# Keeping the low parts of the weights in DRAM instead of computing them again in every chunk

## The reference

```python
h = _layer_norm(x) * (1 + scale[:, None]) + shift[:, None]
proj = h @ w_in                                   # (2048, 1024) @ (1024, 2560)
xa, ga, u, v, gb = jnp.split(proj, SPLITS, axis=-1)
ya = _pool_mixer(xa, w_pool, pool_scale) * jax.nn.silu(ga)
yb = _sgu_mixer(gelu(u), gelu(v), sgu_ln_g, sgu_ln_b, w_sgu, b_sgu) * jax.nn.silu(gb)
y = jnp.concatenate([ya, yb], axis=-1) @ w_out    # (2048, 1024) @ (1024, 1024)
z = DEEPNORM_ALPHA * x + gate[:, None] * y
return _layer_norm(z) * ln_g + ln_b
```

## Time and profile before

| | us |
|---|---|
| median of 3 runs | 678.67 (677.87 to 679.04) |
| profiled execution, its own time | 678.93 |
| span of the profiled execution | 677.2 |
| TensorE busy | 664.5 |
| VectorE busy | 525.6 |
| ScalarE busy | 239.3 |

### The profile page before, as it was taken

How to read it: one execution, slowest core, us unless ns; L and a number is a source line. 1 busy time by engine, 2 the same in 40 slices (tenths; PEclk the granted TensorE clock), 3 DMA queues, 4 the chain that set the end, 5 groups by cost and what they waited for, 6 DMA issues and landing times.

```text
span 677.2 us, 8864 instructions
## 1 busy us (share of the span) xinstructions
PE 664.5 (98%) x3087; PEld 552.9 (82%) x3087; DVE 525.6 (78%) x973; ACT 239.3 (35%) x316; POOL 61.9 (9%) x77
## 2 busy tenths in 40 slices
PE   8999999999999999999999999999999999999995
PEld 7888787878888888888888888888888888888884
DVE  5879989859769868759969967776978977555876
ACT  4444434338213333326511333334721333323300
POOL 2000200100012101100002201000002210000010
PEclk9999999999999999999999999999999999999998
DMA  8993352883425442575324362288233463224011
GB/s 332 396 370 131 125 187 88 169 300 129 142 76 186 168 176 93 97 210 223 126 94 155 124 248 93 93 109 324 93 124 123 136 245 117 95 81 162 38 63 62
DMA packets 33976, 106.68 MB, mean 158 GB/s; under 512 B 6509, under 2 KB 7569, under 8 KB 33938
## 3 DMA queue, kind: packets, MB, share of 16 engines
q1 hardware_dynamic: 33938, 106.22, 47.6%
HBM read 97.80 MB, written 8.40 MB: 157 GB/s over the span
## 4 chain that ended last, share of the span: by engine, by line
PE 89%; DVE 5%; issue 3%; ACT 1%; DMA 1%; POOL 0%; SPq 0%; POOLq 0%; DVEq 0%; ACTq 0%
PE bank_b L1008 59%; PE bank_a L1008 26%; PE bank_a L1122 2%; DVE gate_rows L723 1%; DMA x_norm<-in_x 1%; PE bank_b L1068 1%; DVE x_stats L622 1%; PE bank_b L1032 0%; ACT h_high L476 0%; ACT w_high L466 0%; DVE w_low L601 0%; DVE y_low L829 0%; PE bank_b L1087 0%; PE bank_b L1059 0%; DVE mixed L818 0%
## 5 line engine op out<-in xcount | busy, mean ns | idle before, releaser
L1008 PE MATMUL bank_b<-h_high,w_high 128*128 128x512 f32 x512 | 202.1, 395 | 0.6 <-DVE sgu_bias L757 0.6
L1008 PE MATMUL bank_b<-h_low,w_high 128*128 128x512 f32 x512 | 199.4, 390 | 0.0
L1008 PE MATMUL bank_b<-h_high,w_low 128*128 128x512 f32 x512 | 199.4, 389 | 0.0
L466 ACT ACTIVATE w_high<-w_float 128x1024 fp32r<-128x1024 f32 x100 | 105.5, 1056 | 149.5 <-DMA w_float<-in_w_units 56.3
L601 DVE TENSOR_TENSOR w_low<-w_float,w_high 128x1024 fp32r<-128x1024 f32 x100 | 122.1, 1221 | 42.5 <-ACT w_high L466 42.3
L1008 PEld LDWEIGHTS bank_b<-h_high,w_high 128*128 128x128 f32 x512 | 96.2, 188 | 21.0 <-issue 1.8
L1008 PEld LDWEIGHTS bank_b<-h_high,w_low 128*128 128x128 f32 x512 | 96.1, 188 | 20.2
L1008 PEld LDWEIGHTS bank_b<-h_low,w_high 128*128 128x128 f32 x512 | 96.2, 188 | 19.7 <-issue 0.5
L411 POOL TENSOR_TENSOR z_rstd<-z_var_eps,minus_half 128x1 f32<-128x1 f32 x16 | 22.0, 1377 | 367.3 <-DVE z_var_eps L858 357.4
L1008 PE MATMUL bank_a<-w_high,y_high 128*128 128x512 f32 x128 | 49.8, 389 | 0.0
L1008 PE MATMUL bank_a<-w_low,y_high 128*128 128x512 f32 x128 | 49.8, 389 | 0.0
(11 more groups left out here) (180 smaller groups left out, 945.4 us busy)
## 6 DMA issues: line engine op xcount, KB each, us to landing
w_float<-in_w_units SPq DMA_DIRECT2D x104, 512.0 KB, 3.3
x_norm<-in_x SPq DMA_DIRECT2D x16, 512.0 KB, 4.4
z<-in_x SPq DMA_DIRECT2D x16, 512.0 KB, 5.5
out<-z SPq DMA_DIRECT2D x15, 512.0 KB, 4.7
z<-in_mod_units SPq DMA_DIRECT2D x12, 512.0 KB, 9.6
x_norm<-in_x_channels SPq DMA_DIRECT2D x12, 512.0 KB, 13.8
mod_spare<-in_mod_units SPq DMA_DIRECT2D x6, 512.0 KB, 8.2
x_norm<-in_w_units SPq DMA_DIRECT2D x4, 512.0 KB, 4.3
```

The costliest lines, as they stand in the source:

```text
L466: nc.scalar.activation(wH[:, n % S_SLOTS, :], wF[:, n % F_SLOTS, :], ACT.Copy).then_inc(w_high, 1)
L1008: last = mm(bank, wl if n == 2 else wh, ml if n == 1 else mh, start=start and n == 0, stop=stop and n == 2)
```

## The change

In chunk 0 VectorE still subtracts, and SP stores each of the 28 low parts to a new DRAM tensor `low_units` (`store_low`). In the other chunks SP loads the low part of unit n + 2 in step n straight into its slot of `wL` (`load_low`), and VectorE no longer subtracts there, except for units 20 to 27 of the last chunk, which are prepared as before. SP's load of a weight waits for ScalarE's `w_high_ready` instead of VectorE's `w_low_ready`, and TensorE waits for `w_high_ready` and for the landing. The table `LAST_SPLITS_IN`, the tiles and all products stay as they are.

```diff
+    low_units = nc.dram_tensor("low_units", [UNITS, P, D], F32).ap()
             def load_w(c, n):
-                wait(sp, w_low, c * UNITS + n - F_SLOTS + 1)
+                held = n - F_SLOTS
+                if isinstance(c, int) and c * UNITS + held < UNITS:
+                    wait(sp, w_low, held + 1)
+                elif isinstance(c, int) and c == CHUNKS - 1 and held >= IN_UNITS:
+                    sp.wait_ge(w_low, UNITS + held - IN_UNITS + 1)
+                else:
+                    sp.wait_ge(w_high, c * UNITS + held + 1)
                 sp.dma_start(wF[:, n % F_SLOTS, :], w_units[n % UNITS]).then_inc(w_landed[n % F_SLOTS], 16)
+            def store_low(n):
+                sp.wait_ge(w_low, max(n + 1, len(EARLY)))
+                stored = v_low_stored if n < V_UNITS else low_stored[n % S_SLOTS]
+                sp.dma_start(low_units[n], w_of(0, n)[1].bitcast(F32)).then_inc(stored, 16)
+
+            def load_low(c, n):
+                if n % UNITS < S_SLOTS:
+                    sp.wait_ge(low_stored[n % S_SLOTS], (UNITS // S_SLOTS - 1) * 16)
+                    if isinstance(c, int) and c == 0:
+                        sp.wait_ge(v_low_stored, V_UNITS * 16)
+                sp.wait_ge(unit_done, c * UNITS + n - S_SLOTS + 1)
+                sp.dma_start(wL[:, n % S_SLOTS, :].bitcast(F32), low_units[n % UNITS]).then_inc(low_landed[n % S_SLOTS], 16)
...
                         load_w(c, n + 2 * AHEAD)
+                    if first and V_UNITS < n < FIRST_LOOP:
+                        for unit in ((4, 5, 6, 7), (0, 1), (2, 3))[n - V_UNITS - 1]:
+                            store_low(unit)
+                    if first and FIRST_LOOP <= n + AHEAD < UNITS:
+                        store_low(n + AHEAD)
+                    if (first and n + AHEAD >= UNITS) or (not first and not last) or (last and n + AHEAD < IN_UNITS):
+                        load_low(c, n + AHEAD)
...
+                            if g == 0 and not first:
+                                act.wait_ge(z_stats, c * TILES)
...
             def split_low(c, n):
                 dve.wait_ge(w_high, c * UNITS + n + 1)
+                if isinstance(c, int) and c == 0:
+                    dve.wait_ge(low_stored[n % S_SLOTS], (n // S_SLOTS - 1) * 16)
...
-                    if not (last and n in LAST_SPLITS_IN):
+                    if first and n + AHEAD < UNITS:
                         split_low(c, n + AHEAD)
...
-                    pe.wait_ge(w_low, c * UNITS + n + 1)
+                    if first:
+                        pe.wait_ge(w_low, n + 1)
+                    else:
+                        pe.wait_ge(w_high, c * UNITS + n + 1)
+                        pe.wait_ge(low_landed[n % S_SLOTS], ((c - 1) * (UNITS // S_SLOTS) + n // S_SLOTS + 1) * 16)
```

More of the change, by code:

```diff
@@ L180, in hybrid_layer @@
         unit_done = sem("unit_done")
+        low_stored = [sem(f"w_low_stored{i}") for i in range(S_SLOTS)]
+        v_low_stored = sem("v_w_low_stored")
+        low_landed = [sem(f"w_low_landed{i}") for i in range(S_SLOTS)]
         vec_turned, vec_ready = sem("vec_turned"), sem("vec_ready")
@@ L828, in y_low @@
                 dve.wait_ge(high, c * G + g + 1)
+                if isinstance(c, int) and c == 0 and g == 0:
+                    dve.wait_ge(v_low_stored, V_UNITS * 16)
                 vec.tensor_tensor(yL[:, row, :], src[:, :], yH[:, row, :].bitcast(F32), ALU.subtract).then_inc(low, 1)
@@ L1248, in last_products @@
                             pe.wait_ge(ys_low, c * G + i + 1)
-                            pe.wait_ge(w_low, c * UNITS + IN_UNITS + i + 1)
+                            pe.wait_ge(w_low, UNITS + i + 1)
                         if half == 1 and j == 0:
```

## The result

The changed kernel takes 687.47 us (median of 4 runs, 685.36 to 688.33), the kernel before in the same session 678.86 us. The ratio is 1.0125, with a 95% interval of 1.0099 to 1.0151. The forecast was 680.7 with a range of 678.2 to 683.6: the sign is right, the size is not.

What follows compares the result with a forecast made beforehand. The prediction took TensorE as the bound, busy 98% of the span. To 678.93 us it added 0 for VectorE, 2.0 for unit 19 and 0 for chunk 0: 680.9 profiled, median 680.7, range 678.2 to 683.6.

Steps and rivals of the forecast that it cites:

- What is removed: 76 VectorE subtractions in chunks 1 to 3, 92.8 us of VectorE's work, give the span 0 us.
- Where it does not fit: Unit 19's low part, queued behind the scattered statistics stores, lands late in chunks 1 and 2: 2.0 us, bounds 1.3 to 3.8.
- I take 1.0 of the 1.28 us: Unit 20's weight lands before the stores, so the jam may move ahead by up to 1.28 us; 1.0 was counted.
- the upper bound: If unit 21's weight keeps its time, TensorE stalls at unit 19 for 2.3 us in chunk 1, 1.5 in chunk 2.
- the restart of TensorE: Starting TensorE again after the stall at unit 19 costs 0.1 us, twice.
- Chunk 0: A low-part store moves the jam back 1.28 us; y_pool's reserve before unit 20 is 2.5 us, so 0 was counted.
- signs of being wrong: No TensorE wait for the low part's landing, that wait away from units 19 and 20, or a chunk 0 y_pool wait.
- VectorE's waits for stores cost 0: VectorE's added waits are for stores four units old, which it finds past: 0 us.
- What is late next: Unit 20's low part comes 5.1 us after unit 19's, 0.3 us before it is needed: no second stall, no reserve.
- The pile-up: Rival: the queue drains slower, making unit 20's low part late: 684 us in the middle, 687.3 at the far end; chance 0.13.
- The stall: Main case: TensorE stalls at unit 19 in chunks 1 and 2; own range 680.0 to 683 us, chance 0.50.
- the hidden case: Rival: low parts are hidden everywhere, no loss: 678.7 us and up to 1.3 more; chance 0.33.

Runs made afterwards that it cites:

- experiment 1: The changed kernel without its stores and loads of low parts and the waits for them, multiplying by stale low parts: 678.45 us, ratio 1.0002.
- experiment 5: The kernel before plus chunk 0's 28 stores of low parts; none is loaded and VectorE subtracts in every chunk: 681.93 us, ratio 1.0036.
- experiment 6: The changed kernel with all four loads of x moved from step 16 to 17, behind unit 21's weight and unit 19's low part: 689.72 us, ratio 1.015.
- experiment 8: The changed kernel with the eight early low parts all stored in step 5 of chunk 0, none in steps 6 and 7: 690.21 us, ratio 1.0144.
- experiment 7: The changed kernel with eight unused matmuls ahead of TensorE's wait for unit 19's low part in chunks 1 and 2: 686.87 us, ratio 1.0103.

## Why the prediction was wrong

**What is removed: right.** 0 us for VectorE's subtractions (experiment 1).

**Where it does not fit: the right place, too small.** The term was 2.0 us, with bounds 1.3 and 3.8; the stalls are 3.6 and 1.4 us. The step that failed is "I take 1.0 of the 1.28 us": the room in front of the stores was taken as a gain for all that follows. The stores did land 0.6 and 2.8 us earlier against TensorE, but the weight of unit 21 did not, as the drain from their landing to its rounding grew by 1.9 and 2.7 us. In chunk 2 the weight kept its place, and the stall is 1.4 us, near the 1.5 of the upper bound. In chunk 1 it was 1.3 us later against TensorE than before: the upper bound "if that keeps its time" was no bound. The 0.78 MB that had moved less by 301 us account for the 1.9 us of chunk 1.

Why they were held up more is not settled. Before, the stores' writes ran beside the bytes of a weight issued at 283.46; here the queue had nothing left to move from 284.7 on, and the writes ran alone. That SP's issue blocks needs no low part: it took 10.73 us in experiment 1 too, and in chunk 2 of the changed kernel the four loads took 2.00 us and the one low part behind them 6.91. And the jam varies by itself: from the second store's issue to unit 21's rounding it is 18.4 to 20.3 us in the three kernels without loads of low parts (before, experiments 1 and 5, chunks 1 and 2), and 19.2 and 21.3 us in the changed one. A term worked out to tenths of a microsecond could not be had from one trace of it.

**A missing term: the clock.** 2.9 us behind the stall of chunk 1. The prediction priced the restart of TensorE at 0.1 us, by the wait of 1.0 us in the earlier trace rows. This held for the short waits (unit 19 of chunk 2: 5.69 for 5.46) and not for that of 3.4. Experiments 6 and 8 show the same fall behind 3.1, 3.4 and 4.0 us, experiment 7 none behind 1.3. Around 2 us it went either way: the clock fell a microsecond after the 2.1 us of experiment 6, and it didn't behind the 2.0 us of experiment 8's chunk 2 and the 2.2 and 2.5 us of experiment 7. So the length of the idle time alone doesn't decide it there. The Trainium skill's page "TensorE: Matmul & The Clock Gate", section "What's actually happening", says that the slow clock is the default and that activity releases it; this trace agrees, with 0.50 behind the long wait and 0.99 once TensorE has worked again for a while. The four executions of the changed kernel follow it too: from 688.33 us at a mean clock of 0.991 to 685.36 us at 0.998.

**Chunk 0: 0 was wrong, it cost 1.3 us.** It varies, too: the two waits are 4.7 us in the profile of experiment 7, whose chunk 0 is the same. The reserve of 2.5 us and the path through `y_pool` were right, and TensorE's wait for it is one of the signs of being wrong that the prediction named. What was mis-sized is the delay: the weight of unit 21 is 147.19 - 143.62 = 3.6 us late, not 1.28, and 3.6 - 2.5 = 1.1 us is the wait. Most of it is the jam itself: the second store of the statistics lands 14.5 us after its issue at 126.33, where before it took 11.2 from 125.74. "VectorE's waits for stores cost 0" held, as far as no wait of TensorE ends with one; what was missed is that stores ahead of weights in the same queue delay the weights, and lengthen the wait for pooled_low (experiment 8).

**What is late next: right here.** No second stall at unit 20. With 5.1 us of transfers it was the tight place: experiment 6 put four more loads in front of it, and it broke.

**The rivals.** The pile-up, given 0.13, comes within 0.2 us of the measured time at its far end (687.3), but not by its mechanism: from 301 to 307 us the queue drained at 405 to 419 GB/s, and unit 20 had no second stall. The stall, given 0.50, has the mechanism, and the measured time lies 4.5 us above its own range. Nothing was hidden (0.33): in both chunks it was late.

**The range and the other signs.** The range was said to run from the middle of the hidden case to the middle of the pile-up. By the prediction's own numbers these are 679.4 and 684, and the stated ends are 678.2 and 683.6; the measured time lies above both. The bytes came out right (161.18 MB for 161). TensorE's busy time did not stay within 1 us: the 3.0 us more are nearly all the slower clock. The second store of the statistics took 10.3 to 14.5 us to land, over the three chunks, for the 11 to 13 that were expected.

## What to carry to other kernels

A transfer moved into a full queue costs nothing until it stands behind the one thing that holds the queue up; look for the stretch where the GB/s fall, list all that is queued behind it, and compare each with when it is needed. A stall of TensorE of some 3 us is to be priced together with the slower clock behind it, which nearly doubles it here. Where the profile names what ended a wait, read the program for everything that is waited for there, and compare the times: both new waits had the wrong name here. Putting such a transfer ahead of the bulk loads, using its data last, or storing in longer runs each took the loss of chunks 1 and 2 away alone, but with VectorE off the path there was nothing to win to begin with.

## What was not expected of the hardware

Behind two stores of 2 KB in 1024 writes of 4 bytes the queue moves 13 to 21 GB/s for 8 us of chunk 1, and in the changed kernel the second store lands 10.3 to 14.5 us after its issue; with 256 writes the two land in 1.4 and 3.4 us there. An issue of SP can block for most of that time: 11.70 us for four loads, against some 2 us in the kernel before. And behind each of the four idle times of 3.1 to 4.0 us TensorE's clock was at 1.2 GHz in place of 2.4, while its share of busy time went on to read 100%.
